# Column sums, the silu of conditioning rows and two norm roots moved, a shared weight slot for two short blocks, and two low parts on GpSimd

## What is computed

```python
sh1, sc1, gt1, sh2, sc2, gt2 = split(silu(c) @ w_ada[i] + b_ada[i], 6)
h = rms_norm(x, norm_mix[i]) * (1 + sc1) + sh1
mix = gla_mixer(h, ...) if i == 0 else diff_attention(h, ...)
x = x + gt1 * mix
h = rms_norm(x, norm_ffn[i]) * (1 + sc2) + sh2
up = h @ w_in                      # (T, 2 * D_FF)
conv = conv_b + sum(conv_w[j] * padded[:, j:j + T] for j in range(3))
u, gate = split(conv, 2)
x = x + gt2 * ((silu(gate) * u) @ w_out)
```

## Time and profile before

| | us |
|---|---|
| Median of 3 runs | 1453.94 |
| Lowest, highest | 1451.04, 1454.84 |
| Profiled execution | 1451.93 |
| Its span in the profile | 1449.8 |
| TensorE busy | 1403.0 |
| VectorE, ScalarE, GpSimd busy | 946.6, 653.0, 89.8 |

### The profile page before, as it was taken

One profiled execution on the slowest core, in us unless ns is written; L12 is line 12 of the kernel. 1 busy time (PEld: TensorE's weight loads), 2 busy tenths in 40 slices (PEclk: granted clock), 3 DMA queues, 4 the chain that ended last, 5 costly groups with the idle time before them and its releaser, 6 DMA issues.

```text
span 1449.8 us, 26539 instructions
## 1 busy us (share of the span) xinstructions
PE 1403.0 (97%) x11024; PEld 1319.4 (91%) x11024; DVE 946.6 (65%) x1559; ACT 653.0 (45%) x1454; POOL 89.8 (6%) x153
## 2 busy tenths in 40 slices
PE   8999999999999999999899999999899999999999
PEld 6888877989999899999898887879799999999999
DVE  4577676467787887978675555465778755455454
ACT  4543343346555155242365555553475552552421
POOL 0000000110000100100200000000300000000000
PEclk9999999999999999999999999999999999999999
DMA  9434433133343643635332222112324313223213
GB/s 379 154 117 142 135 124 124 66 117 113 135 146 114 217 149 109 228 130 166 129 122 86 75 74 99 63 56 82 117 85 148 117 67 105 89 70 105 78 61 106
DMA packets 36388, 173.98 MB, mean 120 GB/s; under 512 B 4108, under 2 KB 6284, under 8 KB 25901
## 3 DMA queue, kind: packets, MB, share of 16 engines
q1 hardware_dynamic: 21356, 118.52, 23.4%
q0 software_dynamic: 14912, 53.78, 10.7%
HBM read 164.37 MB, written 7.91 MB: 119 GB/s over the span
## 4 chain that ended last, share of the span: by engine, by line
PE 84%; DVE 7%; ACT 4%; issue 3%; DMA 2%; POOL 0%; DVEq 0%; SPq 0%; POOLq 0%; ACTq 0%
PE ps L582 25%; PE ps L584 24%; PE ps L583 24%; DVE w_lo L1526 2%; ACT w_hi L1066 2%; PE ps L968 1%; PE ps L1010 1%; PE ps L620 1%; DMA a_raw<-in_ada_r 1%; PE ps L922 1%; DVE xT L1682 1%; DVE sq L1598 1%; PE ps L988 1%; DVE h_lo L1611 1%; DVE a_prod L1558 1%
## 5 line engine op out<-in xcount | busy, mean ns | idle before, releaser
L582 PE MATMUL ps<-h_hi,w_hi 128*128 128x272 f32 x2080 | 611.7, 294 | 20.1 <-ACT new_conv L1363 6.3
L584 PE MATMUL ps<-h_hi,w_lo 128*128 128x272 f32 x2080 | 605.2, 291 | 0.0
L583 PE MATMUL ps<-h_lo,w_hi 128*128 128x272 f32 x2080 | 601.9, 289 | 0.0
L582 PEld LDWEIGHTS ps<-h_hi,w_hi 128*128 128x128 f32 x2080 | 395.4, 190 | 32.1 <-issue 9.1
L583 PEld LDWEIGHTS ps<-h_lo,w_hi 128*128 128x128 f32 x2080 | 396.0, 190 | 1.3 <-issue 1.0
L584 PEld LDWEIGHTS ps<-h_hi,w_lo 128*128 128x128 f32 x2080 | 394.7, 190 | 0.0
L1526 DVE TENSOR_TENSOR w_lo<-w_raw,w_hi 128x2048 fp32r<-128x2048 f32 (+2 forms) x109 | 226.7, 2080 | 81.7 <-ACT w_hi L1066 81.5
L1066 ACT CAST w_hi<-w_raw 128x2048 fp32r<-128x2048 f32 (+2 forms) x109 | 188.3, 1728 | 202.9 <-PE ps L584 171.7
L582 PE MATMUL ps<-act_hi,w_hi 128*128 128x272 f32 (+1 forms) x704 | 203.7, 289 | 2.5 <-DVE xT L1682 1.5
L583 PE MATMUL ps<-act_lo,w_hi 128*128 128x272 f32 (+1 forms) x704 | 203.8, 290 | 0.0
L584 PE MATMUL ps<-act_hi,w_lo 128*128 128x272 f32 (+1 forms) x704 | 203.2, 289 | 0.0
(11 more groups left out here) (267 smaller groups left out, 1657.6 us busy)
## 6 DMA issues: line engine op xcount, KB each, us to landing
w_raw<-in_wst SPq DMA_DIRECT2D x73, 1024.0 KB, 4.8
a_raw<-in_ada_r POOLq DMA_DIRECT2D x56, 512.5 KB, 4.0
w_raw<-in_wst SPq DMA_DIRECT2D x28, 768.0 KB, 4.2
a_raw<-in_ada_g POOLq DMA_DIRECT2D x24, 512.0 KB, 3.5
a_pro<-in_ada_w SPq DMA_DIRECT2D x8, 1024.0 KB, 18.1
w_raw<-in_wst SPq DMA_DIRECT2D x8, 512.0 KB, 3.4
xT<-in_xT SPq DMA_DIRECT2D x4, 544.0 KB, 7.1
out<-kT POOLq DMA_DIRECT2D x4, 544.0 KB, 3.0
```

Of the source, the lines that this page charges most:

```text
L582: mm(out, lhs_hi, rhs_hi, start=first, stop=False)
L583: mm(out, lhs_hi, rhs_lo, start=False, stop=False)
L584: return mm(out, lhs_lo, rhs_hi, start=False, stop=last)
```

## The change

1. **Banks.** The third up block of each layer's chunk 0 (`("up", l, 0, 2)`) puts its four units in banks 4, 5, 7, 6, no longer 0, 1, 2, 3.
2. **Column sums.** In `first_pair` the half-1 sums stand after k = 5, no longer after k = 1; before the second FFN the half-0 sums stand two units later.
3. **Shared slot.** The blocks down 0,3,2 and down 0,3,3 (4 k tiles each) lie side by side in one slot of `w_hi`. The slots behind them change places, and dk0 can be cast when down 0,3,1 is finished.
4. **Change of layer.** The cast of dk0 moves ahead of the last half-0 square, its low part ahead of the last three stream updates; squares and tiles take turns one by one.
5. **GpSimd.** The low parts of dq0 and of the second up block of layer 1 are made by GpSimd, behind its sums.
6. **Silu of the rows.** ScalarE's silu of `c_row` moves from the first gate tile to the start of `ffn(l)`.
7. **Row pieces.** No piece behind the last unit of a down block; two pieces, no longer one, in the gate up blocks.
8. **Before the second FFN.** ScalarE's half root comes one square earlier, squares and tiles take turns in another way; VectorE makes one more update ahead of the first half tile.

```diff
@@ place_units
+        elif kind == "up" and BL[n][2:] == (0, 2):
+            b = (4, 5, 7, 6)[u - FIRST_U[n]]
+SHARED = BN[("down", 0, 3, 3)]
+def hi_slot(n):
+    if n == SHARED:
+        return (n - 1) % 2, CH[3] * BC
+    return (n + 1 if n > SHARED else n) % 2, 0
@@ gpsimd
+            def low(n):
+                pool.wait_ge(w_hi_ok, n + 1)
+                pool.wait_ge(w_lo_ok, n)
+                slot, at = hi_slot(n)
+                m = block_kt(n) * BC
+                pool.tensor_tensor(w_lo[:, n % 3, 0:m], w_raw[:, n % 3, 0:m], f32(w_hi[:, slot, at:at + m]), ALU.subtract).then_inc(w_lo_ok, 1)
             sum_tiles(2)
+            low(BN[("dq", 0)])
...
             sum_tiles(3)
+            low(BN[("up", 1, 0, 1)])
@@ tensor, first_pair
-                        if half == 0 and k == 1:
+                        if half == 0 and k == 5:
                             stats(which, 1)
@@ tensor, output projection
-            units(DOUT_B[0:KT + 3])
+            units(DOUT_B[0:KT + 5])
             stats(3, 0)
@@ scalar, split
-                    act.wait_ge(unit_done, LAST_U[n - 2] + 1)
+                    act.wait_ge(unit_done, LAST_U[n - 3 if n == SHARED + 1 else n - 2] + 1)
-                act.copy(w_hi[:, n % 2, 0:m], w_raw[:, n % 3, 0:m]).then_inc(w_hi_ok, 1)
+                slot, at = hi_slot(n)
+                act.copy(w_hi[:, slot, at:at + m], w_raw[:, n % 3, 0:m]).then_inc(w_hi_ok, 1)
@@ scalar, squares_of
-                for m in range(4, KT):
+                for m in range(4, KT - 1):
                     square(which, m, 0)
+                if which == 2:
+                    split(n + 4)
+                square(which, 7, 0)
                 square(which, 4, 1)
                 half_root(which, 0)
...
                     half_modulated(which, 0, (0,))
-                    split(n + 4)
                     square(which, 5, 1)
+                    half_modulated(which, 0, (1,))
                     square(which, 6, 1)
-                    half_modulated(which, 0, (1,))
+                    half_modulated(which, 0, (2, 3))
                     square(which, 7, 1)
-                    half_modulated(which, 0, (2, 3))
                     split(n + 5)
@@ scalar, ffn
+                act.wait_ge(crow_in, 48 + 16 * l)
+                A_(c_row[:, :, 0:D], c_row[:, :, 0:D], ACT.Silu).then_inc(crow_ok, 1)
                 for kind, c in FFN_ORDER:
...
-                                if tile == 2 * FT * l + 3:
-                                    act.wait_ge(crow_in, 48 + 16 * l)
-                                    A_(c_row[:, :, 0:D], c_row[:, :, 0:D], ACT.Silu).then_inc(crow_ok, 1)
@@ scalar, before the second FFN
-            for m in range(4):
+            for m in range(3):
                 square(3, m, 1)
             half_root(3, 0)
             half_modulated(3, 0, (0,))
+            square(3, 3, 1)
             square(3, 4, 1)
+            half_modulated(3, 0, (1,))
             square(3, 5, 1)
-            half_modulated(3, 0, (1,))
             square(3, 6, 1)
+            half_modulated(3, 0, (2,))
             square(3, 7, 1)
-            half_modulated(3, 0, (2, 3))
+            half_modulated(3, 0, (3,))
             split(BN[("up", 1, 0, 1)])
@@ vector, stage_end (which == 2)
+                    low(n + 2)
                     out(us[5])
-                    half_tiles(which, 0, (0,))
+                    half_tiles(which, 0, (0, 1))
                     out(us[6])
-                    low(n + 2)
+                    half_tiles(which, 0, (2, 3))
                     out(us[7])
-                    half_tiles(which, 0, range(1, KT))
-                    low(n + 3)
+                    half_tiles(which, 0, range(4, KT))
@@ vector, row pieces
-                    if rows:
+                    if rows and u != LAST_U[n]:
                         ada_rows(FFN_ROWS_DONE)
...
-                            for _ in range(2 - j if t >= j and rows_from <= ub < rows_to else 0):
+                            for _ in range(2 if t >= j and rows_from <= ub < rows_to else 0):
@@ vector, before the second FFN
-            last_out(DOUT_B[KT:KT + 4])
+            last_out(DOUT_B[KT:KT + 5])
             half_tiles(3, 0, (0,))
-            last_out(DOUT_B[KT + 4:KT + 6])
+            last_out(DOUT_B[KT + 5:KT + 7])
             half_tiles(3, 0, (1,))
-            last_out(DOUT_B[KT + 6:])
+            last_out(DOUT_B[KT + 7:])
             half_tiles(3, 0, range(2, KT))
-            low(BN[("up", 1, 0, 1)])
             half_tiles(3, 1, range(KT))
```

8 lines of the change are left out of this document (5 added, 3 removed).

## The result

The changed kernel took 1463.94 us (median of 7 runs, 1460.72 to 1467.05) against 1453.94 us before (7 runs, 1451.04 to 1457.62); the ratio of the runs is 1.0059, with a 95% interval of 1.0045 to 1.0074. The forecast was 1452.5, its range 1442 to 1458: the time lies outside it, on the side to which I had given 0.15.

The account below looks back on a forecast made before the run. TensorE, busy 1403.0 of 1449.8 us, bounds the kernel; only its 46.8 us idle and lower-clock stretches can be won. Terms -5.5 - 1.8 + 4.7 + 1.2 = -1.4 us gave 1452.5 against the 1453.94 median, range 1442 to 1458.

Parts of the forecast that it names:

- First FFN's beginning: First FFN's start: later sums, moved silu and free banks remove TensorE's waits and a slow stretch, -5.5 us.
- Step (3): First FFN, third up block: free banks remove the 3.16 us wait, and nothing of it returns at the fourth block.
- Step (1): First FFN: sums after six tiles gain 0.8 us before the pair's second block, later eaten by the third block's low part.
- Step (2): First FFN: silu and table load move to where ScalarE waits for TensorE; chain behind starts 0.1 to 0.2 us later, not 3.2.
- The 0.4 kept back: First FFN: 0.4 us held off the 5.9 gain, since TensorE may leave its waits between 309.4 and 313.9 at the lower clock.
- Row pieces: FFN blocks: removing pieces from down blocks gives -3.3 us, adding them to up blocks +1.5; together -1.8 us.
- So 0.5 us, at three chunks: Last up block ahead of each down chunk: one more piece delays the first stream update, 0.5 us each, +1.5 in all.
- Change of layer: Up to dk0 and dq0: GpSimd's 4.6 us pass blocks VectorE, +2.4 us, plus 2.3 for the lower clock; +4.7 us.
- Rival A: GpSimd does not hold VectorE up for the whole pass, at both places: sum -12.3, 1441.6 us; chance 0.13.
- rival C: GpSimd's pass writes the rounded type slowly, extending both places; at 9.2 us 1461.7, middle of case 1459.3; chance 0.12.
- rival B: GpSimd blocks, but the clock is kinder behind the long waits and the chunks' new waits are absorbed: 1446.4 us; chance 0.20.
- Second FFN's beginning: Output projection's end and second FFN's start: +1.4 and +2.3 for the clock, then -2.5 from the removed bank wait; +1.2 us.

Follow-up runs that it names:

- b1: The kernel before with only the new banks 4, 5, 7, 6 of each layer's third up block: 1447.95 us, ratio 0.9945.
- c1: b4 with the half-1 column sums after two tiles again in every first pair: 1440.28 us, ratio 0.9898 against the kernel before.
- b4: Changed kernel with low parts back on VectorE and the ten pieces given up by down blocks behind act_lo: 1441.66 us, ratio 0.9896 against the kernel before.
- a2: Changed kernel with both GpSimd low parts back on VectorE: 1456.14 us, ratio 1.0007 against the kernel before.
- b3: The kernel before with only the silu of c_row moved to the start of the FFN: 1453.55 us, ratio 0.9988.
- a4: The kernel before with only the new places of the row pieces: 1461.90 us, ratio 1.0042.
- a1: Changed kernel with the row pieces placed as before: 1453.39 us, ratio 0.9992 against the kernel before.
- b5: a1 with each GpSimd low part made by four instructions of 512 columns: 1450.20 us, ratio 0.9962 against the kernel before.
- c3: b4 with the order ahead of the second FFN as in the kernel before: 1443.14 us, ratio 0.9910 against the kernel before.
- d1: The kernel before with the new banks and the new places of the row pieces: 1458.34 us, ratio 1.0026.

## Why the forecast failed, step by step

**First FFN's beginning** (-5.5): right in sum, and in mechanism for the banks: -6.3. Step (3) holds by b1. Step (1), 0.8 us gained and eaten again, holds by c1 against b4 (1.2 and 0.9). The changed kernel's own execution shows neither (-0.2 in 303-316): behind its wait of 1.80 us at 312.20 the granted clock was 0.72 (31 matmuls in 6.00 us), where a2 had 31 in 5.10 us at 1.00 and then waited 0.83 us for a low part. Step (2) was right that the silu costs nothing in its new place; its 3.2 us were mis-sized, 0.9 by b3, since ScalarE had waited for VectorE there anyway. The 0.4 kept back was for such a clock; it came, and cost nothing, since it fell into time that was lost in any case.

**Row pieces** (-1.8, measured +11.4): this is the step that failed. The part removed was right (-3.3 forecast, -3.7 measured in 474-500). Counted in the traces, the down blocks have 46 pieces before and 36 after, so ten went to gate up blocks, not twelve. The part added failed, in two steps. "The twelve pieces go to up blocks, where VectorE has room" was read from VectorE's idle time. The idle time is there (in 347 to 468 VectorE was busy 95.9 of 121 us), but the pieces stood ahead of the product, in a chain through both engines that has 0.37 us to spare in a pair, against a piece of 1.22. And "So 0.5 us, at three chunks" counted only the last piece of each run of blocks. What comes out at a chunk's first unit is the lag that its pairs have gathered: 3.19 us behind five pairs, 2.05 behind three, 1.14 behind two, and behind the first two a slower clock as well (0.51 and 0.71). These were +3.9 and +6.1, +3.7 and +1.4 us where the sum had 1.5, and +2.2 in the second layer, whose pieces were to "hide in VectorE's idle time". I had walked through each place with TensorE at its old time, although my first term had just moved TensorE 5 us forward. Both errors have a size: at TensorE's old time (a4) the term is 5.4 us in place of -1.8, so 7.2 of its miss of 13.2 are the chain's, and the other 6, with the 2.2 of the second layer, come with the lead.

**Change of layer** (+4.7): right: +4.2 in 671-738. Point by point: the pass took 4.50 us (4.6 forecast), the step behind it ended 0.3 us after it (0.3 forecast), TensorE waited 6.63 us (5 to 7), and then ran with a granted clock of 0.57, for which 2.3 us had been charged from the earlier trace rows. Here is the stretch behind the wait; columns as in the earlier trace rows:

```profile
738.00:744.00 6.00, 5.83 (x24) 5.37 (x25) 2.45 (x6) 1.90 (x4) 2.47 (x7) 0.57 0.66 229
```

and the same stretch in a1:

```profile
727.20:733.20 6.00, 6.00 (x24) 5.54 (x24) 2.39 (x6) 1.96 (x4) 2.33 (x6) 0.53 0.70 240
```

In both, 24 matmuls in 6.00 us cost 6.00 - 24 x 0.126 = 3.0 us, near the upper end of my 1.5 to 3.1. Rival A (no full block) fell by the step of 4.41 us, rival C (a slow write) by the 4.50 us, rival B (a kinder clock, the chunks' waits absorbed) by this stretch and by the chunks. GPSIMD Engine Reference of the Trainium skill (Elementwise — side-by-side cycle accounting) has 4497 ns for an add of 2048 float32 columns; the mean of the two passes here, which subtract and write fp32r, is 4496. The Trainium skill's page SBUF — State Buffer (SBUF: two separate sides) says that the one of VectorE and GpSimd that starts first holds the shared pair of ports for the whole instruction and the other fully blocks, for VectorE instructions with two SBUF inputs against GpSimd ones that read SBUF too; the 4.41 us and b5's four turns agree.

**Second FFN's beginning** (+1.2, measured -0.1): 1028-1052 came out at +2.5 where the sum had 1.4 + 2.3 = 3.7. The pass held VectorE's step up as was said (4.42 us, and a wait of TensorE of 4.84 at 1056.95), but the new order ahead of it gave 2.4 us (c3), not 1.5, and the slow stretch cost 6.00 - 32 x 0.126 = 2.0 us (granted clock 0.72 in 1057 to 1063). The gain behind it was 2.6, as forecast (2.5), though TensorE's remaining wait there was not the third block's low part but 0.55 us for `up` at 1075.27.

The range failed with the one term: the added pieces had no upper bound of their own, though no row showed them behind the banks' lead. Had I bounded them by the extra piece in every pair, 10 x 1.22 us (an estimate), the range would have reached 1465.

## What to carry to other kernels

Before an operation is put where an engine "has room", follow the chain that it stands in, through all engines, over one period of the loop: what counts is the spare time of the chain (here 0.37 us in 24.16), not the idle share of the engine. An early step of a change that moves the bottleneck engine forward takes away the slack in which the later steps were to hide, so that two edits which are each cheap may cost more together: redo the timeline from the moved times. Work of no urgency goes behind the last operation that others wait for, and work given to GpSimd beside a VectorE that is on the path goes in short instructions, or not at all.

## What the hardware showed

VectorE, in its steps with two SBUF inputs, and GpSimd take turns instruction by instruction (b5): four quarters and four VectorE steps interleaved; steps of 0.50 us took 1.18 to 1.50, and the pass 5.55 in place of 4.50, in part for its number of instructions.

The clock after a wait was not a function of the wait. The same wait for the same update, of 3.18 to 3.21 us, was followed by half clock in the changed kernel and a2 (28 matmuls in 6.00 us), by a mixed stretch in d1, and by full clock in a4 (columns as in the earlier trace rows). The changed kernel:

```profile
471.00:477.00 6.00, 5.99 (x27) 6.00 (x27) 6.00 (x12) 0.07 (x1) 0.53 (x1) 0.51 0.58 197
```

d1:

```profile
472.00:478.00 6.00, 6.00 (x36) 6.00 (x37) 6.00 (x12) 0.00 (x0) 0.53 (x1) 0.72 0.53 193
```

and a4:

```profile
475.50:481.50 6.00, 6.00 (x48) 6.00 (x49) 6.00 (x12) 0.01 (x1) 0.53 (x1) 1.00 0.59 197
```

These are 27, 36 and 48 matmuls in 6.00 us. In the changed kernel and d1 TensorE had waited four times in the 100 us before, in a4 once for 0.43 us. Whether that is the reason was not tried; d1, with nearly the same waits as the changed kernel and another clock behind them, speaks against it as the whole reason. It makes 2 to 3 us of what a wait costs uncertain, as much as the wait itself.
